# Two transformer blocks in one kernel: the activation tiles at a pitch of 1280 bytes, and the activation and weight tiles begun 128 bytes past a multiple of 256

## The reference, cut to what matters

```python
h = rmsnorm(x, pre_mix_g);  proj = h @ w_in                 # 2048 x 9984: q, k, v of three mixers, then three gates
mix = ga * (ya @ w_oa) + gb * (yb @ w_ob) + gc * (yc @ w_oc)  # three branches, 512 x 2048 each
x = x + rmsnorm(mix @ w_out, post_mix_g)                    # 2048 x 2048
u = rmsnorm(x, pre_ffn_g) @ w_up                            # 2048 x 11264, then a 3-tap convolution over tokens
x = x + rmsnorm((gelu(gate) * val) @ w_down, post_ffn_g)    # 5632 x 2048
# second block: 16 meta tokens are put ahead of the 256
y = rmsnorm_2(h, pre_norm[0]);  proj = y @ attn_w_in        # 2048 x 6144, 16 heads of attention, gated
h = h + rmsnorm_2((o * silu(gate)) @ attn_w_out, post_norm[0])
y = rmsnorm_2(h, pre_norm[1]);  proj = y @ gla_w_in         # 2048 x 6176, gated linear attention both ways
h = h + rmsnorm_2((o * silu(g_out)) @ gla_w_out, post_norm[1])
```

## The kernel before, in words

| operand | start | pitch | starts mod 256, before |
|---|---|---|---|
| slices of `whi`, `wlo` | 32960, 49344 | 512 | 192 |
| tiles of `ahi`, `alo` | 65792, 84224 | 1152 | 0 for even k, 128 for odd k |
| tiles of `yhi`, `ylo` | 183296, 195584 | 1024 | 0 |
| tiles of `ghi`, `glo` | 131200, 176256 | 1024 (512 per half) | 128 |
| tiles of `z2hi_first`, `z2lo_first` | 220416, 224768 | 1088 | 0, 64, 128, 192 for k = 0 to 3 |
| tiles of `z0hi`, `z0lo` | 191552, 195648 | 1024 | 64 |

## Time and profile before

### The profile page before, as it was taken

How to read it: one execution, slowest core, us unless ns; L and a number is a source line. 1 busy time by engine, 2 the same in 40 slices (tenths; PEclk the granted TensorE clock), 3 DMA queues, 4 the chain that set the end, 5 groups by cost and what they waited for, 6 DMA issues and landing times.

```text
span 2430.8 us, 43574 instructions
## 1 busy us (share of the span) xinstructions
PE 2357.6 (97%) x17033; PEld 2187.8 (90%) x17033; DVE 1410.4 (58%) x1814; ACT 1171.0 (48%) x1739; POOL 246.7 (10%) x202
## 2 busy tenths in 40 slices
PE   8999999999989999999999989999999989999998
PEld 7897899998879999999988869998889989998876
DVE  5555644458566666666655557885554463555544
ACT  5444544445454554454444444444455453664443
POOL 0000000015002211221200001220002000010210
PEclk9999999999999999999999989999999989999999
DMA  8544466656646556556666645443335555553343
GB/s 288 155 138 133 134 195 185 186 156 192 206 139 191 185 178 198 188 177 196 207 190 191 191 145 163 149 150 118 102 99 175 172 163 166 151 156 104 106 165 138
DMA packets 254406, 402.37 MB, mean 166 GB/s; under 512 B 15135, under 2 KB 111388, under 8 KB 253244
## 3 DMA queue, kind: packets, MB, share of 16 engines
q1 hardware_dynamic: 252452, 393.53, 52.6%
q10 hardware_dynamic: 1832, 7.13, 0.9%
HBM read 396.38 MB, written 4.22 MB: 165 GB/s over the span
## 4 chain that ended last, share of the span: by engine, by line
PE 91%; DVE 4%; ACT 3%; issue 2%; POOL 0%; DMA 0%; ACTq 0%; DVEq 0%; POOLq 0%; SPq 0%
PE bank L1758 62%; PE bank L1855 13%; PE bank L2281 4%; PE bank L1773 2%; DVE wlo L1132 2%; ACT whi L570 1%; PE bank L2247 1%; PE bank L2072 1%; PE bank L2041 1%; PE bank L1798 1%; PE bank L2208 1%; PE bank L2016 0%; PE bank L2010 0%; DVE mixtmp L1420 0%; PE bank L1920 0%
## 5 line engine op out<-in xcount | busy, mean ns | idle before, releaser
L1132 DVE TENSOR_TENSOR wlo<-raw,whi 128x1024 fp32r<-128x1024 f32 x749 | 953.2, 1282 | 815.0 <-ACT whi L570 811.6
L1758 PE MATMUL bank<-ahi,whi 128*128 128x256 f32 (+1 forms) x4224 | 1210.6, 287 | 2.8 <-ACT gg L892 1.0
L1758 PE MATMUL bank<-alo,whi 128*128 128x256 f32 (+1 forms) x4224 | 1195.0, 283 | 0.0
L1758 PE MATMUL bank<-ahi,wlo 128*128 128x256 f32 (+1 forms) x4224 | 1193.1, 282 | 0.0
L570 ACT ACTIVATE whi<-raw 128x1024 fp32r<-128x1024 f32 x749 | 787.4, 1057 | 782.0 <-PE bank L1758 548.7
L1758 PEld LDWEIGHTS bank<-ahi,whi 128*128 128x128 f32 x4224 | 796.9, 189 | 20.0 <-issue 17.1
L1758 PEld LDWEIGHTS bank<-alo,whi 128*128 128x128 f32 x4224 | 796.6, 189 | 1.4 <-issue 0.2
L1758 PEld LDWEIGHTS bank<-ahi,wlo 128*128 128x128 f32 x4224 | 795.6, 188 | 0.0
L1855 PE MATMUL bank<-wlo,ghi 128*128 128x512 f32 x352 | 138.7, 394 | 0.0
L1855 PE MATMUL bank<-whi,glo 128*128 128x512 f32 x352 | 138.0, 392 | 0.0
L1855 PE MATMUL bank<-whi,ghi 128*128 128x512 f32 x352 | 136.6, 388 | 0.0
(11 more groups left out here) (305 smaller groups left out, 2299.9 us busy)
## 6 DMA issues: line engine op xcount, KB each, us to landing
raw<-in_w_up SPq DMA_DIRECT2D x176, 512.0 KB, 3.8
raw<-in_w_in SPq DMA_DIRECT2D x156, 512.0 KB, 3.8
raw<-in_attn_w_in SPq DMA_DIRECT2D x96, 512.0 KB, 4.0
raw<-in_gla_w_in SPq DMA_DIRECT2D x96, 512.0 KB, 3.8
raw<-in_w_down SPq DMA_DIRECT2D x80, 512.0 KB, 4.2
raw<-in_w_out SPq DMA_DIRECT2D x32, 512.0 KB, 4.5
raw<-in_attn_w_out SPq DMA_DIRECT2D x32, 512.0 KB, 3.7
raw<-in_gla_w_out SPq DMA_DIRECT2D x32, 512.0 KB, 3.7
```

What stands on the lines that cost most here:

```text
L1132: dve.tensor_tensor(wlo[:, u % RING, :], raw[:, u % RAW, :], whi[:, u % RING, :].bitcast(F32), ALU.subtract).then_inc(wlo_ready, 1)
L1758: mm = pe.matmul(bank[:, base + t, 0:T], w[wp][:, k, col:col + P], rhs(ap, k0 + k), start=begins and k == 0 and (wp, ap) == (0, 0), stop=e ...
```

## The change

The diff moves tiles and nothing else. `AS` becomes 320 elements, so that the pitch of an activation tile is 1280 bytes, five times 256. Small tiles (`lam`, `qkgain`, `ynsum`, `xstat`) go ahead of `whi`, which puts it at 33152, `wlo` at 49536, `ahi` at 65920 and `alo` at 86400. `R2`, the base of the regions, becomes an address that is 128 modulo 256 (135296). The `z2` tiles get the pitch of 1280 as well, with 128 bytes of padding ahead, and `z0hi` moves by 192 bytes more. After it, every start of a weight slice and of an activation tile in the table above is 128 modulo 256.

Room for this is found by two overlays: the FFN's `cv` moves into `tmp`, and the attention probabilities `p2` move to where `cos`, `sin`, `turn`, `sq2` and a part of `rs2` lie. `gain2`, `yn2` and the rest of the tiles laid over `ahi` and `alo` follow `AS`.

```diff
-AS = (T2 + 31) // 32 * 32
+AS = 320
...
         raw = sb("raw", [P, RAW, UNIT])
+        lam = sb("lam", [P, 8])
+        subg = lam[:, 4:5]
+        eps = lam[:, 5:6]
+        qkgain = sb("qkgain", [P, 24])
+        ynsum = sb("ynsum", [P, 2, 4])
+        xstat = sb("xstat", [P, 4, 2])
         whi = sb("whi", [P, RING, UNIT], F32R)
         wlo = sb("wlo", [P, RING, UNIT], F32R)
-        place_at[0] = act_at = (place_at[0] + 255) // 256 * 256
+        act_at = place_at[0]
+        assert act_at % 256 == 128
...
-        R2 = (place_at[0] + 255) // 256 * 256
+        R2 = place_at[0] + (128 - place_at[0]) % 256
...
-        ghi, glo, cv, pr = region(("ghi", [P, FT, TB], F32R), ("glo", [P, FT, TB], F32R), ("cv", [P, 4, TB], F32),
-                                  ("pr", [P, 2, TB], F32), base=R2 + 128)
+        ghi, glo, pr = region(("ghi", [P, FT, TB], F32R), ("glo", [P, FT, TB], F32R), ("pr", [P, 2, TB], F32))
+        cv = sb("cv", [P, 4, TB], F32, at_=tmp_at)
...
-            ("z2hi_first", [P, FIRST_GATED, T2], F32R), ("z2lo_first", [P, FIRST_GATED, T2], F32R))
+            ("z2_pad", [P, 32], F32), ("z2hi_first", [P, FIRST_GATED, AS], F32R), ("z2lo_first", [P, FIRST_GATED, AS], F32R))
+
+        p2 = sb("p2", [P, 2, 3, T2], F32, at_=R2 + 4 * (24 * T2 + 3 * 1024 + KD * T2))
...
-        z0_at = R2 + 4 * (16 * T2 + 3 * D + KD * TB + 2 * P + T2)
+        z0_at = R2 + 4 * (16 * T2 + 3 * D + KD * TB + 2 * P + T2) + 192
...
-                return (z2hi_first, z2lo_first)[part][:, h, :]
+                return (z2hi_first, z2lo_first)[part][:, h, 0:T2]
```

More of the change, by code:

```diff
@@ L160, in two_blocks_kernel @@
         ones = sb("ones", [P, P])
[L161 to L164, removed]
         cum_at = place_at[0]
@@ L170, in two_blocks_kernel @@
         xm = sb("xm", [P, KD, TM])
-        ynsum = sb("ynsum", [P, 2, 4])
-        xstat = sb("xstat", [P, 4, 2])
         tmp_at = place_at[0]
@@ L227, in two_blocks_kernel @@
         (yT,) = region(("yT", [P, KD, T2], F32))
-        ghi, glo, cv, pr = region(("ghi", [P, FT, TB], F32R), ("glo", [P, FT, TB], F32R), ("cv", [P, 4, TB], F32),
-                                  ("pr", [P, 2, TB], F32), base=R2 + 128)
+        ghi, glo, pr = region(("ghi", [P, FT, TB], F32R), ("glo", [P, FT, TB], F32R), ("pr", [P, 2, TB], F32))
+        cv = sb("cv", [P, 4, TB], F32, at_=tmp_at)
         FIRST_GATED = 4
-        qk2, v2, gs2, cos, sin, turn, sq2, rs2, n2, nc2, p2, pT2, nm2, sum2, vt2, z2hi_first, z2lo_first = region(
+        qk2, v2, gs2, cos, sin, turn, sq2, rs2, n2, nc2, pT2, nm2, sum2, vt2, _, z2hi_first, z2lo_first = region(
             ("qk2", [P, 24, T2], F32), ("v2", [P, 3, 1024], F32), ("gs2", [P, KD, T2], F32), ("cos", [P, T2], F32),
             ("sin", [P, T2], F32), ("turn", [P, P], F32), ("sq2", [P, 2, T2], F32), ("rs2", [P, 2, T2], F32),
-            ("n2", [P, 2, T2], F32), ("nc2", [P, 2, T2], F32), ("p2", [P, 2, 3, T2], F32), ("pT2", [P, 2, 3, T2], F32),
+            ("n2", [P, 2, T2], F32), ("nc2", [P, 2, T2], F32), ("pT2", [P, 2, 3, T2], F32),
             ("nm2", [P, AT_HEADS, 3], F32), ("sum2", [P, AT_HEADS, 3], F32), ("vt2", [P, 2, 4, T2], F32),
-            ("z2hi_first", [P, FIRST_GATED, T2], F32R), ("z2lo_first", [P, FIRST_GATED, T2], F32R))
+            ("z2_pad", [P, 32], F32), ("z2hi_first", [P, FIRST_GATED, AS], F32R), ("z2lo_first", [P, FIRST_GATED, AS], F32R))
+        p2 = sb("p2", [P, 2, 3, T2], F32, at_=R2 + 4 * (24 * T2 + 3 * 1024 + KD * T2))
         (gqk, v3, gg, maskf, maskb, reset, vt3, qdec, kinv, kendf, kendb, kfar, kback, sc, scm, osq3) = region(
```

## The result

The change makes the kernel slower: 2449.68 us (median of four runs, 2448.86 to 2450.62) against 2430.85 us for the kernel before on the same chip, a ratio of 1.0074 with a 95% interval of 1.0061 to 1.0087. The forecast was 2411.3 us, the range 2386 to 2440. The two executions that were profiled took 2449.13 and 2432.57 us, 16.6 apart where the medians are 18.8 apart; what follows by stage accounts for these two.

The account below looks back on a forecast made before the run. The prediction took PE's matmul pace as the bound. Gains of 2.8 + 5.9 + 2.7 + 3.8 + 6.3 = 21.5 us, nine tenths counted as 19.4, gave 2430.7 - 19.4 = 2411.3 us, range 2386 to 2440.

Parts of the forecast that it names:

- What bounds the kernel: Whole kernel: PE's own matmul pace sets the time; PE computes 97% of the span, four matmul lines hold 81% of the chain.
- The wide matmuls: 960 wide matmuls of wout, gout, qkva and qkvc go from about 232.9 to 228.9 ns, gaining 3.8 us; down gains 0.
- The pitch under narrow matmuls: Even activation tiles move from 0 to 128 and cost what odd ones do: gains of 2.8, 5.9 and 2.7 us.
- twice these sums: Upper bound on the narrow matmuls' gain from the pitch, if a run of tiles alike beats either in turn.
- The weights' start: Weight slices move from 192 to 128: 12,672 narrow matmuls gain 0.5 ns each, 6.3 us.
- The upper bound: Worst case for moving the weights: narrow matmuls on `ahi` and `alo` slow to gates' slowest duration, 283 ns.
- The collision: Rival: activations and weights loading beside them, both at 128, meet in every narrow matmul; 33 us lost, 2464 us; chance 0.18.
- Half the price: Half the loss priced for streaming activations and loading weights meeting at equal starts in narrow matmuls: 2447 us.
- No effect: Rival: the even-odd difference belongs to place or turn, not address; with the wide gain alone 2427 to 2431 us; chance 0.17.
- the two pairs of paces: Evidence that starts matter, against the skill's page: 117.9 against 116.7 ns for one form, 232.7 against 228.9 for another.
- The cover: In oabc DVE's conversion sets the end, so the gain is 0; moved tiles elsewhere hide behind DVE's idle 42%.
- The nine tenths: Share of the 21.5 us of saved PE work expected to reach the whole kernel's time: 19.4 us.

Follow-up runs that it names:

- acts_alone: The change with the weights put back to start at 192 modulo 256, activation tiles all at 128: 2398.88 us, ratio 0.9862 to the kernel before.
- wlo_apart: The change with `whi` at 192 and `wlo` left at 128, activations at 128; no total time given, up ran at 117.8 ns a matmul.
- The two sweeps: The change with activation tiles in four groups, moving minus stationary start 0, 64, 128, 192; weights at 128 or 192: 2442.36 and 2444.45 us.
- weights_alone: The kernel before with only the weights moved to 128 modulo 256 (and `p2` over `cos` for room): 2443.19 us, ratio 1.0048.

## Why the prediction was wrong

**What bounds the kernel** was right. PE's pace is the time, and the pieces of the earlier trace rows are where to read it: the stages grew by 16.7 us and the span by 16.5.

**The wide matmuls** moved as forecast and further: from 232.7 to 227.2 ns in wout where 228.9 was expected. Down, left at 0, gained 2.3 us. The reason was not that a start of 128 is good. With the pitch alone, in acts_alone, the gap is 64 everywhere and wout is at 57.80 / 252 = 229.4 ns, near the forecast; the rest came with the weights, which made the gap 0.

**The pitch under narrow matmuls** was put at a gain of 11.4 us with the weights where they were. acts_alone measures this part with the wide one: 34 us instead of 11.4 + 3.8. The step that failed here is the reading of an odd tile's 277 to 281 ns as what an odd tile costs by itself. It was the cost of three matmuls at a gap of 192 with three at 64 on either side; alone, 192 has 113.3 ns. The bound of "twice these sums" was still too small: up alone gained 13.7 us in acts_alone where its term was 2.8.

**The weights' start** is the step that failed and turned the sign. I took a gain of 6.3 us, since both rows with a start of 128, the odd tiles and down, were the quicker ones. That read an address where the rows held a difference: 128 against 192. With the activations all at 128, weights at 192 leave a gap of 192 under every narrow matmul, the best of the eight measured; moving them to 128 as well makes it 0, the worst. Against the gain of 6.3 us it cost about 50, from acts_alone to the change. The upper bound, gates' slowest 283 ns, was the right one, and it is what every narrow matmul over 256 columns now lasts.

**The collision** was the right rival, with its place and its 283 ns. Its full price of 33 us was too high by the step from duration to pace (up was priced at 4.3 ns a matmul, 18.2 us, and lost 3.3 ns, 13.9 us), by the 272-wide matmuls, priced at 8.1 us and in fact nearly unmoved (125.5 ns at a gap of 0 against a mix of 124.3 and 125.9 before), and by the 4.8 us that wout, down and gout gained. Half the price, 2447 us, lies near the measured time, but no row had given a half: that is luck. I had held two rows against it: a z2 tile that starts like the weights and lasts 287, 287 and 286 ns. They are over 272 columns, where a gap of 0 costs next to nothing, and in a pattern of four starts. They could not speak for 256 columns.

**No effect** fell: pieces and span moved. It had one thing right, that something besides the address sets a pattern. The Trainium skill, "TensorE: Matmul & The Clock Gate", Part 2, gives PE two independent read ports. The prediction concluded that a start should then not count, and the runs do not bear that out, with 113.3 against 120.0 ns for the same instructions; what the ports do no run shows. Of the two pairs of paces that the prediction held against it, the first, gates against up, has the same starts on both sides and said nothing of starts.

**The cover** held: DVE's 1,282 ns and oabc's length (73.4 us before, 73.5 after, from its first matmul to the end of its last) did not move. The nine tenths was too low: nearly all of what PE lost reached the span.

What stays open is the mechanism. That the pace of a run of one gap goes by the gap, and not by either start, is shown, with two paces at 192. That the meeting of the streaming operand with the weight load beside it is the cause is only argued, and wlo_apart did not bear out its simplest form. What decides at a break whether a gap of 192 settles at 113.3 or at 117.8 ns is open too.

## What to carry to other kernels

Where matmuls like these follow each other without a break, it is worth a trial to give both operands one pitch that is a multiple of 256 bytes and to choose the difference of their starts, not the starts: here 192 for 256 moving columns and 0 for 512, worth 1.5% of the whole kernel at no instruction. Measure that difference in runs of equal ones long enough to settle; a row out of a mix of differences gives neither its size nor, as here, its sign. A row for one width says nothing for another. And run such a kernel many times, since one layout took 19 to 22 us longer in 4 runs of 11.

## What the runs showed of the hardware

- In runs of one gap a narrow matmul over 256 columns costs 113.3 (gap 192) to 120.0 ns (gap 0), one over 512 columns 226.7 (gap 0) to 233.7 (gap 192): the preferences are opposite. Over 272 columns the spread is 123.6 to 126.5.
- The two sweeps, 64 bytes apart in both operands, agree within 0.1 ns: the absolute starts do not count.
- Sixteen bytes matter: 119.1 ns at a gap of 208, where 192 has 117.8 in the same kernel and 113.3 in others.
- Gaps in turn do not cost the mean of their paces: 118.8 and 120.0 together gave 117.8 in up of weights_alone, 228.9 and 226.7 gave 233.3 in down of wlo_apart.
- The pace is exact where it has settled: 120 ns for matmul after matmul, and pieces of 4,128 that repeat to 0.02 us in kernels with other addresses. Behind a change of the gap from 128 to 192 it took five matmuls.
- The gap of 192 has two patterns, 113.3 and 117.8 ns. A stretch takes up one at a break and keeps it to the next, and the same stretch of the same kernel had one in one execution and the other in another.
